# A gated delta-rule layer on one core: another prologue and another spread of the first body's projection products

## The reference

```
mod = silu(c) @ ada_w + ada_b                    # 3 x 1024
shift, scale, gate = split(mod, 3)
h = rms_norm(x, norm_w) * (1 + scale) + shift
p = h @ w_in                                     # q, k, v, z of 8 heads, and b, a
q, k, v = silu(causal_short_conv(p, conv_w))     # 4 taps; q and k are l2-normed
beta = sigmoid(b);  g = -exp(a_log) * softplus(a + dt_bias)
o = gated delta rule over (q, k, v, beta, g)     # a 256 x 128 state a head
x = x + gate * ((rms_norm(o) * silu(z)) @ w_out)
out = rms_norm(x, final_norm_w)
```

## Time and profile before

| | |
|---|---|
| median of 3 runs | 1266.35 us (1266.05 to 1270.23) |
| profiled execution, own time | 1268.89 us |
| its span, first to last instruction | 1267.1 us |
| PE busy | 1130.3 us, 89% of the span |
| DVE, ACT, POOL busy | 852.0, 453.1, 583.8 us |
| mean granted clock of TensorE | 0.969 |

### The profile page before, as it was taken

The page is one execution under the profiler, slowest core; times in us unless marked ns, Lnnn a source line. Parts: engine busy times, 40 slices in busy tenths (PEclk is TensorE's granted clock), DMA queues, the critical chain, the costliest instruction groups (busy, mean ns, idle before and its releaser), DMA issues.

```text
span 1267.1 us, 19510 instructions
## 1 busy us (share of the span) xinstructions
PE 1130.3 (89%) x5628; PEld 921.6 (73%) x5628; DVE 852.0 (67%) x1896; ACT 453.1 (36%) x1038; POOL 583.8 (46%) x817
## 2 busy tenths in 40 slices
PE   2787699998999989998999989998999989998985
PEld 1665478777787878777787868877787868877763
DVE  3746668585857767585857767585758767585845
ACT  3452233424333332424333342434333432434323
POOL 3114454447444644447344644446344644446413
PEclk9888699999999999999999999999999999999988
DMA  9522331222222231222222231223122131213002
GB/s 302 168 84 76 89 92 38 61 55 67 63 51 51 62 76 38 59 54 76 54 49 52 63 76 38 60 53 84 45 59 54 50 76 45 66 40 92 21 34 117
DMA packets 150754, 88.31 MB, mean 70 GB/s; under 512 B 29446, under 2 KB 145320, under 8 KB 150696
## 3 DMA queue, kind: packets, MB, share of 16 engines
q1 hardware_dynamic: 150696, 87.73, 25.4%
HBM read 78.28 MB, written 9.44 MB: 69 GB/s over the span
## 4 chain that ended last, share of the span: by engine, by line
PE 54%; DVE 13%; POOL 13%; issue 13%; ACT 2%; DMA 2%; SPq 1%; DVEq 1%; POOLq 0%; ACTq 0%
PE bank L401 24%; PE bank L499 14%; POOL w_lo L1317 6%; DVE work L912 4%; POOL wo_lo L1324 3%; DVE y L945 3%; PE bank L545 2%; POOL w_raw L1331 2%; PE bank L459 2%; DMA work<-in_ada_w 2%; DVE gate_bc L1155 1%; PE bank L555 1%; PE bank L558 1%; PE bank L468 1%; PE bank L475 1%
## 5 line engine op out<-in xcount | busy, mean ns | idle before, releaser
L1317 POOL TENSOR_TENSOR w_lo<-w_raw,w_hi 128x256 fp32r<-128x256 f32 x384 | 316.8, 855 | 319.3 <-ACT w_hi L673 319.1
L401 PE MATMUL bank<-h_hi,w_hi 128*128 128x512 f32 x760 | 315.5, 415 | 28.7 <-POOL w_lo L1317 28.7
L401 PE MATMUL bank<-h_hi,w_lo 128*128 128x512 f32 x760 | 311.5, 410 | 0.0
L401 PE MATMUL bank<-h_lo,w_hi 128*128 128x512 f32 x760 | 310.5, 409 | 0.0
L401 PEld LDWEIGHTS bank<-h_hi,w_hi 128*128 128x128 f32 x760 | 144.9, 191 | 60.7 <-POOL w_lo L1317 33.1
L912 DVE SCALAR_TENSOR_TENSOR work<-pre,cw,work 128x512 f32<-128x512 f32 x192 | 173.1, 902 | 15.4 <-DVE work L909 5.4
L401 PEld LDWEIGHTS bank<-h_hi,w_lo 128*128 128x128 f32 x760 | 144.5, 190 | 30.2 <-issue 0.2
L401 PEld LDWEIGHTS bank<-h_lo,w_hi 128*128 128x128 f32 x760 | 144.8, 191 | 28.6
L1367 POOL TENSOR_TENSOR og_lo<-work,og_hi 128x256 fp32r<-128x256 f32 x64 | 47.1, 736 | 223.6 <-ACT og_hi L733 223.6
L699 ACT ACTIVATE work<-work 128x512 f32<-128x512 f32 x64 | 40.5, 633 | 300.3 <-DVE pre L920 143.2
L499 PE MATMUL bank<-wo_hi,og_hi 128*128 128x512 f32 x256 | 113.1, 442 | 16.3 <-DVE y L945 16.3
(11 more groups left out here) (174 smaller groups left out, 1897.3 us busy)
## 6 DMA issues: line engine op xcount, KB each, us to landing
w_raw<-in_gdn_w_in SPq DMA_DIRECT2D x96, 512.0 KB, 4.0
work<-in_ada_w SPq DMA_DIRECT2D x8, 1024.0 KB, 9.3
w_raw<-in_gdn_w_out SPq DMA_DIRECT2D x16, 512.0 KB, 3.3
y<-in_x SPq DMA_DIRECT2D x8, 512.0 KB, 8.1
work<-in_ada_w SPq DMA_DIRECT2D x8, 512.0 KB, 5.1
n_dram<-work SPq DMA_DIRECT2D x16, 256.0 KB, 4.5
out<-y SPq DMA_DIRECT2D x8, 512.0 KB, 2.7
t_dram<-work SPq DMA_DIRECT2D x16, 64.0 KB, 1.6
```

What stands on the lines that cost most here:

```text
L401: mm = nc.tensor.matmul(bank[m % 2][:, :], w[:, m % 2, k, :], h[:, k, half, :], start=(r == 0), stop=(r == MM - 1))
L1317: i = nc.gpsimd.tensor_tensor(w_lo[:, k % 2, j:j + 2, :], w_raw_k[:, k % 2, j:j + 2, :], w_hi[:, k % 2, j:j + 2, :].bitcast(F32), ALU.subt ...
```

## The change

- Scale: the column sums of the scale half of `ada_w` are no longer made by `sum_ada` on DVE with one product on PE each; PE makes them from the raw tile, eight products of one column for each of two columns of `mod`, so `sum_mod` has 18 products where it had 4. `sum_ada` has 256 columns where it had 512.
- The diagonals of the row norms are made by POOL (one instruction a half) and no longer by DVE (four a half).
- `hf`, the float32 copy of h between `make_h` and `split_h`, has four buffers where it had two.
- The gate rows have eight buffers where they had three; their loads come earlier in SP's order, behind the last `load_ada`, and `sum_gate` stands earlier on DVE. SP loads all of x first, and waits for `mod_mm` where it waited for `ada_summed`.
- PE has another order of `turn_x`, `sum_mod` and `project_first`; `gate_mm` stands between tiles 0 and 1 of unit 0. On DVE `invert_blocks(0)` stands behind the sums of `gate_done`, and the last convolution of the prologue, which stood in body 0, behind `invert_blocks(0)`.
- Body 0 has a table of its own, `FILL_FIRST`, that spreads its 96 products over all gaps.

```diff
-        gate_buf = [part(a, 1024) for a in (10752, 11776, 5120)]
+        gate_buf = [part(a, 1024) for a in (11264, 10240, 0, 1024, 2048, 3072, 5120, 6144)]
-        hf = pre[:, :, 3:3 + HALF]
+        hf = [pre[:, 0, 3:3 + HALF], pre[:, 1, 3:3 + HALF], part(9216, HALF), part(9728, HALF)]
...
-        FILL_MERGE = ((12, 12), (10, 10), (6, 6))
-        FILL_V = 16
-        FILL_R = ((8, 8, 6), (8, 8, 6), (2, 2, 6), (2, 2, 6))
-        FILL_TAIL = 8
+        FILLS = (((12, 12), (10, 10), (6, 6)), 16, ((8, 8, 6), (8, 8, 6), (2, 2, 6), (2, 2, 6)), 8)
+        FILL_FIRST = (((8, 8), (6, 2), (4, 4)), 8, ((6, 6, 4), (8, 8, 4), (2, 2, 6), (2, 2, 6)), 0)
...
             def sum_mod(d):
+                if d == 0:
+                    pe.wait_ge(c_step, 3)
+                else:
+                    pe.wait_ge(mod_done, 2 * d)
+                pe.wait_ge(ada_in[d % 2], 32 * (d // 2 + 1))
+                for i in range(2):
+                    col = KT + 2 * d + i
+                    for k in range(KT):
+                        nc.tensor.matmul(bank[5][:, col:col + 1], ada_buf[:, d % 2, k, 1, i * P:(i + 1) * P],
+                                         c_th[:, k:k + 1], start=(k == 0), stop=(k == KT - 1))
                 pe.wait_ge(ada_summed, KT * (d + 1))
...
-            for n in range(2):
+            project(0, 0, 0, MM)
...
-            body(0, 0, begun=BEGUN)
+            project(0, 0, MM, BEGUN)
+            body(0, 0, begun=BEGUN, fills=FILL_FIRST)
...
+                pool.wait_ge(x_pow, half + 1)
+                nc.gpsimd.tensor_tensor(row_scale[:, 4 * half:4 * half + 4, :],
+                                        ident[:, :].unsqueeze(1).to_broadcast([P, 4, P]),
+                                        xrs[:, 4 * half:4 * half + 4].unsqueeze(2).to_broadcast([P, 4, P]), ALU.mult
+                                        ).then_inc(scale_done, 1)
```

More of the change, by code:

```diff
@@ L615, in project_first, with turn_both @@
                     mm.then_inc(ba_mm, 1)
-            turn_x(0, 0)
-            sum_mod(0)
-            turn_x(0, 1)
-            turn_x(1, 0)
-            turn_x(1, 1)
-            for k in range(KT):
-                project_first(k)
-                if k < 6 and k % 2 == 0:
-                    sum_mod(k // 2 + 1)
-                if k < 6:
-                    turn_x(k + 2, 0)
-                    turn_x(k + 2, 1)
+            def turn_both(k):
+                turn_x(k, 0)
+                turn_x(k, 1)
+            turn_both(0)
+            turn_both(1)
+            sum_mod(0)
+            turn_both(2)
+            sum_mod(1)
+            project_first(0)
+            turn_both(3)
+            project_first(1)
+            sum_mod(2)
+            turn_both(4)
+            turn_both(5)
+            sum_mod(3)
+            project_first(2)
+            turn_both(6)
+            project_first(3)
+            turn_both(7)
+            for k in range(4, KT):
+                project_first(k)
             project(-1, 1, 72, 80)
@@ L817, in _, with square_x @@
             nc.scalar.activation(c_th[:, :], c_col, ACT.Tanh, scale=0.5).then_inc(c_step, 1)
-            def square_x(half):
-                for t in range(4 * half, 4 * half + 4):
+            def square_x():
+                for t in range(TILES):
                     act.wait_ge(x_in[t], 16)
@@ L1051, in eps_of_q, with body @@
                                         ALU.mult, ALU.add).then_inc(S["q_eps_done"], 1)
-            def body(hd, par, last=False):
+            def body(hd, par, last=False, first=False):
                 u, other, nxt = 2 * hd + par, 1 - par, hd + par
@@ L1245, in _ @@
             silu(-1, 3, cvq[:, 0, :])
-            for k in range(3):
-                sum_gate(k)
-            invert_blocks(0, 0, BLK - 1)
             conv(-1, 1, 0, 2)
-            for k in range(3, KT):
-                sum_gate(k)
             attn(0)
-            dve.wait_ge(gate_summed, KT)
-            spread_t(0)
             dve.wait_ge(gate_mm, 1)
@@ L1259, in _ @@
                                         gate_bias[:, n * 512:(n + 1) * 512], ALU.add).then_inc(gate_done, 1)
-            body(0, 0)
+            invert_blocks(0, 0, BLK - 1)
+            silu(-1, 4, cvv[:, 0, :])
+            conv(-1, 1, 0, 3)
+            spread_t(0)
+            body(0, 0, first=True)
             with dve.Fori(0, HEADS - 1) as hd:
```

141 lines of the change are left out of this document (70 added, 71 removed).

## The result

The changed kernel took 1284.1 us (median of 4 runs, 1283.49 to 1285.29), beside 1268.3 for the kernel before on the same chip: a ratio of 1.0136, interval 1.0116 to 1.0157. It is slower, as forecast, but by 1.36%, about twice what was forecast: 1276.0 us would be 0.6% above 1268.3, and the sum of +9.7 us is 0.8%. The time lies in the range, near its upper end. The profiled execution took 1285.29 us with a span of 1282.5.

A forecast was written before the change was run, and what follows sets the result against it. PE was taken to bound the kernel, with only prologue and body 0 changing: -0.5 (first stage) + 5.2 (tables, inversion) + 1.6 (front) + 3.4 (rest) = +9.7 us on the median of 1266.35, giving 1276.0 us, range 1261 to 1286.

The forecast's parts named there:

- First stage: Prologue to the end of `project_first(7)`: about even, ending at 80.8 us instead of 81.35, a gain of 0.5.
- T: End of the first stage, that is of `project_first(7)`; 81.35 us in the kernel before.
- The rivals with T' near 70 and near 90: New first-stage end T': full clock near 70, about 1266 us (0.22); one-column products keeping clock down near 90, 1285 (0.13).
- half clock: PE's granted clock of 0.50, assumed for mostly the early first stage, since 40 to 48 us showed it while busy.
- Tables and inversion: From T over `g_tab` and `n_done` to the end of `invert_blocks(0)`: 5.2 us later, seen from T.
- B: End of `invert_blocks(0)`; 122.58 us in the kernel before.
- PE's `turn_k` covers 1.1 of it: In the tables: of `g_tab`'s 4.6 us delay `turn_k` hides 1.1, so `n_done` is 3.5 later.
- Front and rest of body 0: Front, B to K, 1.6 us later; rest, K to body 1, 3.4 us later.
- the waits: In body 0, PE waits for POOL's `w_lo`: some 9 us for tile 3, then two of about 4 in chunks 0 and 1.
- K: Start of the first product of chunk 0 in body 0; 166.44 us in the kernel before, forecast at B + 45.5.
- Sum: All four pieces to body 1: -0.5 + 5.2 + 1.6 + 3.4 = +9.7 us, median 1276.0 us.
- The first one: Body 0 rival: `w_lo` of tiles 3 to 5 beats PE, earlier start kept, -3.7 to -8, some 1260 us; chance 0.12.

The follow-up runs named there:

- the run with new fills in the kernel before: Kernel before, with body 0's fills spread nearly as in the changed kernel: 1287.8 us, ratio 1.0150 to the kernel before.
- The last run: Changed kernel with body 0's earlier fills, inversion ahead of the adds, gate steps 0 to 6 in DVE's first-stage idle time: 1241.7 us, ratio 0.9820 to the kernel before.
- the fills alone: Changed kernel with body 0's fills put back as they lay before, also the run that removed the waits: 1258.2 us, ratio 0.9921 to the kernel before.
- The run with sixteen extra products: Changed kernel plus 16 unused 512-column products on PE behind body 0's first merge: 1281.7 us, ratio 1.0102 to the kernel before.
- all three edits: Changed kernel with body 0's earlier fills, inversion ahead of attn(0) and the adds, gate steps 3 to 7 later: 1248.6 us, ratio 0.9848 to the kernel before.
- middle fills: Changed kernel with a body 0 spread between old and new, 12 tile 2 products among the merges: 1262.7 us, ratio 0.9974 to the kernel before.
- 10 extra products: The version with all three edits plus 10 unused 512-column products behind body 0's first two merge_p and merge_d: 1249.2 us, ratio 0.9871 to the kernel before.

## Why the prediction was right or wrong

**First stage: the gain was larger than forecast.** Forecast a gain of 0.5, measured 3.8. PE does run nearly without idle time from 20 us on and sets the stage, as put. But `sum_mod(0)` started at 25.18 where I had 28.0, and I had counted it at 5.4 us and the second at 7.2, half clock; with their last four instructions they took 4.7 and 4.6 (from 25.18 and 35.39), nearer the full price of 3.6. That makes 6 us, and 3 of them were lost again behind: above all `sum_mod(3)` took 5.5 us, not 3.6, and the second projection with the `turn_x` ahead of it 4.5, not 3.6. The profiles scatter here too: with its first stage unchanged, the run with new fills in the kernel before ended it at 80.0 instead of 81.35, and with the changed one T lies between 77.2 and 78.8, so the gain is 1.2 to 4.2. The rivals with T' near 70 and near 90 didn't happen. The clock wasn't full, although PE had no gap over 2.1 us from 20 us on: 0.80 and 0.76 in the two stretches above. The stretch from 40 to 48 us on which I based half clock was weaker evidence than this one, since an idle gap of 5.34 us lay right ahead of it.

**Tables and inversion: right steps, 3.4 us too cheap.** Forecast T to B +5.2, measured +8.6 (49.8 us for 41.2). The order was as read from the code: three steps ahead of `g_tab`, the inversion behind the adds. The sizes were off: a step took 1.70 us, not 1.35, beside POOL's `split_lo`, and 1.28 to 1.35 elsewhere; and PE, which then waited 6.08 us, did the products behind it at half clock. "PE's `turn_k` covers 1.1 of it" was wrong: `n_done` was 7.3 later seen from T, not 3.5 (6.0 to 7.5 over the profiles). The last run shows that all of it belongs to the steps' places. The other part, `n_done` to B, was forecast at 24.0 and took 23.6.

**Front and rest of body 0: the waits right, the clock behind them missed.** The waits were forecast at about 9, 4 and 4 us and came as 7.11, 3.89 and 4.53; that they appear and vanish with the fills alone is shown from both sides. But B to K took 51.0 us where I had 45.5 (K was B + 43.9 before), and K to body 1 51.1 where I had 45.7 (42.3 before): +7.1 and +8.8 for +1.6 and +3.4. This is the step that failed: the terms of the sum between and behind the waits were too small. I gave half clock to the first eight products behind the first wait and to four behind the second, and full clock to the merges between and to all behind the third and fourth wait; the rows show 0.50 from 131 to 151 and from 165 to 175 us, and below 1.00 up to 206. The run with sixteen extra products gives about 5 us of body 0 for the first of these stretches alone.

The clock isn't all of it. Of the 5.5 us missed up to K, 2.2 lie ahead of the first wait's end: `w_lo` of tile 2 came at B + 14.4 where I had B + 12.2, since `w_out` had landed only at B + 8.9, not B + 6.6. From there to the second `merge_p` it was 10.0 us for 7.1, at half clock; the first convolution ended at B + 29.5 (I had B + 24.5), and `w_lo` of tile 3 came at B + 41.9 (B + 37.5). Of the 5.4 missed behind K, 2.4 lie in the chain from `w_lo` of tile 4 to that of tile 5, 15.1 us for 12.7, and the rest in what PE did behind the waits. What lengthened that chain was not tried apart. Two sums are also 0.2 us off their own terms (K is B + 45.3, body 1 K + 45.5), which changes nothing here.

**Sum.** +20.7 us at body 1 for +9.7. At the end 15.8 are left between the medians. In the profiles the spans differ by 15.4, so 5.3 of the 20.7 us are gone by then. The fifteen later bodies don't differ by a mechanism that I found: in each profile those with even numbers take either 71.4 to 72.6 or 73.2 to 74.2 us, what follows the start of the last body takes either 63.0 to 63.3 or 64.7 to 65.0, and how often the longer times come differs from one execution to the next (five in the profile of before, three in that of after). That explains 3 to 4 of the 5.3 us; the cause of the two lengths stays open.

**The rivals.** The first one (the wait for tile 3 costs nothing) put the fills' harm at some 11 us; it is 26 (the fills alone). Its sum doesn't follow from its own terms: +9.7 less 8 and less 3.4 is -1.7, some 1264.6, not -3.7 to -8. That its figure of some 1260 is close to the 1258.2 of the run that removed the waits is luck, and that run got there by another order of the fills, not by an earlier `w_lo`.

## What to carry to other kernels

Before products are moved ahead in an in-order queue, find out when their operand is ready, and place them by that: here 16 more products ahead of chunk 0 turned slack of POOL's chain into idle time of the bounding engine, and putting only the old fills back made a loss of 1.4% a gain of 0.8%. Cheap work on a second engine belongs in its idle stretches, not beside its critical steps: the same eight steps put the tables off by 6 to 7.5 us in one place and by nothing in another. And follow the queue of SP: what looked like a wait of POOL for DVE's adds was a load queued behind a write that waited for the inversion.

## What the runs showed of the hardware

- A wait of TensorE can cost more than its length: behind one of 6.42 us the granted clock stayed at 0.50 for another 9 us of products (142 to 151 us), and with sixteen products in the wait it was 1.00 there, 4.2 us saved up to the next merge. The Trainium skill ("TensorE: Matmul & The Clock Gate", section "Why this matters for your kernels") says that idle gaps lose the full clock; here the trace agrees. Not each wait does it: behind one of 1.05 us (all three edits) and one of 2.82 us (middle fills) the clock stayed at 1.00, behind one of 2.65 us (10 extra products) it fell to 0.50.
- But a busy TensorE isn't always at full clock: it was busy 20.00 of 20.00 us from 40 to 60 us of the changed kernel at a mean granted 0.76, where each fall came within or just behind a group of one-column products, and 15.6 of 16.4 us in a stretch of 64-column products mixed with a few wide ones at a granted 0.58. By that section's rule both would have had the full clock after their start; here the measurement decides. No run tried the width of the products by itself.
- A step of DVE with two SBUF operands took 1.70 us beside POOL's `split_lo` and 1.28 to 1.35 us elsewhere, and the `split_lo` beside it 5.99 us where the same form takes 2.77 alone (138.97 us). The Trainium skill ("GPSIMD Engine Reference", section "1. Specifications") lists the SBUF interfaces as shared with VectorE for instructions with two SBUF inputs; the trace agrees.
